# Changing the order of ranking, routing and row scoring in a product-key expert kernel, and where two normalisations end

## The reference, cut to what matters

```python
q = (xt @ w_query).reshape(t, PEER_HEADS, 2, PEER_KEY_DIM // 2)
s = jnp.einsum('thpd,hpkd->thpk', q, sub_keys)
s_half, i_half = lax.top_k(s, PEER_TOPK)                       # 16 of 128 keys, twice
cand = s_half[:, :, 0, :, None] + s_half[:, :, 1, None, :]
top_s, top_pos = lax.top_k(cand.reshape(t, PEER_HEADS, 256), PEER_TOPK)
experts = take_along_axis(cand_idx, top_pos)                   # 8 heads x 16 = 128 per token
gates = softmax(top_s)
a = gelu(einsum('tkd,td->tk', expert_u[experts], x), approximate=False)
y = einsum('tk,tkd->td', gates * a, expert_v[experts])
x = layer_norm(ALPHA * x + ga2 * y, ln2_g, ln2_b)
```

## Time and profile before

| | us |
|---|---|
| median of 3 runs | 1932.91 |
| lowest, highest | 1929.52, 1939.39 |
| the profiled execution, its own time | 1945.27 |
| its span, first to last instruction | 1943.5 |
| PE busy | 1795.4 (92%) |
| DVE busy | 1292.2 (66%) |
| POOL busy | 896.7 (46%) |
| DMA share, mean rate | 345 GB/s over the span |

### The profile page before, as it was taken

One profiled execution on the slowest core, in us unless ns is written; L12 is line 12 of the kernel. 1 busy time (PEld: TensorE's weight loads), 2 busy tenths in 40 slices (PEclk: granted clock), 3 DMA queues, 4 the chain that ended last, 5 costly groups with the idle time before them and its releaser, 6 DMA issues.

```text
span 1943.5 us, 21544 instructions
## 1 busy us (share of the span) xinstructions
PE 1795.4 (92%) x8020; PEld 1152.3 (59%) x8020; DVE 1292.2 (66%) x2593; ACT 293.5 (15%) x661; POOL 896.7 (46%) x837
## 2 busy tenths in 40 slices
PE   4988898998999999998999999996889999999994
PEld 1666743554444359987888888884554444444441
DVE  2110476989579699998998975568875623336767
ACT  0120010555100001111111100005550000000000
POOL 1010225665456324334455555668865665435540
PEclk9999999999999999998999999998999999999998
DMA  8895859888999977559999999999989999999995
GB/s 360 338 370 214 344 160 394 291 286 324 392 324 363 390 272 298 187 192 362 366 361 375 386 387 409 405 394 329 327 308 409 409 409 409 409 409 409 409 410 203
DMA packets 168441, 670.21 MB, mean 345 GB/s; under 512 B 19563, under 2 KB 19691, under 8 KB 163085
## 3 DMA queue, kind: packets, MB, share of 16 engines
q0 software_dynamic: 112512, 410.79, 56.2%
q1 hardware_dynamic: 51072, 242.25, 31.8%
q10 hardware_dynamic: 4752, 15.81, 2.1%
HBM read 659.27 MB, written 7.39 MB: 343 GB/s over the span
## 4 chain that ended last, share of the span: by engine, by line
PE 46%; DMA 18%; DVE 18%; POOL 11%; issue 6%; ACT 1%; ACTq 0%; DVEq 0%; another core or an unknown queue 0%; POOLq 0%
PE psum L966 19%; POOL arena L566 11%; DMA arena<-in_expert_u_dram,arena 9%; DMA arena<-in_expert_v_dram,arena 4%; DVE arena L1511 4%; PE psum L751 4%; PE psum L992 3%; PE psum L995 3%; DVE psum L1784 3%; PE psum L740 2%; PE psum L1029 2%; DVE arena L1707 2%; DMA arena<-in_w_ada_dram 2%; PE psum L1006 2%; PE psum L1004 2%
## 5 line engine op out<-in xcount | busy, mean ns | idle before, releaser
L566 POOL DMA_INDIRECT arena<-in_expert_u_dram,arena x384 | 468.5, 1220 | 386.0 <-DVE arena L1511 261.6
L1511 DVE CUSTOM_DVE_ANT_0 arena<-arena 128x1024 f32<-128x1024 f32 x384 | 461.0, 1222 | 182.1 <-DMA arena<-in_expert_u_dram,arena 153.0
L566 POOL DMA_INDIRECT arena<-in_expert_v_dram,arena x384 | 390.7, 1018 | 357.9 <-DVE psum L1784 175.9
L1784 DVE SCALAR_TENSOR_TENSOR psum<-arena,psum 128x1024 f32<-128x1024 f32 x254 | 327.0, 1287 | 193.2 <-DMA arena<-in_expert_v_dram,arena 165.0
L893 PE MATMUL psum<-arena 128*128 128x256 f32 x2048 | 446.0, 381 | 7.3 <-DMA arena<-in_expert_uT_dram 7.3
L966 PE MATMUL psum<-arena 128*128 128x512 f32 x1024 | 443.7, 594 | 1.6 <-DMA arena<-in_expert_v_dram 1.6
L893 PEld LDWEIGHTS psum<-arena 128*128 128x128 f32 x2048 | 390.8, 191 | 61.3 <-issue 7.6
L966 PEld LDWEIGHTS psum<-arena 128*128 128x128 f32 x1024 | 193.3, 190 | 253.0 <-issue 249.0
L1064 PE MATMUL psum<-arena 128*128 128x128 f32 x1280 | 148.9, 278 | 2.1 <-DVE arena L1668 1.4
L1064 PEld LDWEIGHTS psum<-arena 128*128 128x128 f32 x1280 | 147.1, 194 | 3.6 <-issue 1.9
L1324 ACT ACTIVATE arena<-psum 128x512 f32<-128x512 f32 x64 | 38.2, 597 | 379.7 <-PE psum L893 292.6
(11 more groups left out here) (188 smaller groups left out, 1410.1 us busy)
## 6 DMA issues: line engine op xcount, KB each, us to landing
arena<-in_expert_uT_dram SPq DMA_DIRECT2D x128, 512.0 KB
arena<-in_expert_v_dram SPq DMA_DIRECT2D x128, 512.0 KB
arena<-in_w_ada_dram SPq DMA_DIRECT2D x12, 2048.0 KB
arena<-in_w_in_dram SPq DMA_DIRECT2D x11, 2048.0 KB
arena<-in_w_query_dram SPq DMA_DIRECT2D x8, 2048.0 KB, 22.7
arena<-in_w_in_dram SPq DMA_DIRECT2D x30, 512.0 KB, 7.9
arena<-in_w_o_dram SPq DMA_DIRECT2D x4, 2048.0 KB
arena<-in_expert_u_dram,arena POOLq DMA_INDIRECT x384
```

What stands on the lines that cost most here:

```text
L566: pool.indirect_dma_start(slot, None, table[0], bass.IndirectOffsetOnAxis(ap=number, axis=0)).then_inc(land, 16)
L1511: dve.tensor_tensor_reduce(UR[b], UR[b], U2B[e], 1.0, 0.0, ALU.mult, ALU.add, DOTS[e % 2][:, k:k + 1]).then_inc(u_free, 1)
L1784: dve.scalar_tensor_tensor(ys, row, weight, ys, ALU.mult, ALU.add).then_inc(v_free, 1)
```

## The change: what it does

Tile 4 is queried, ranked and routed after tile 2. Groups of rows are dealt between 25 of the 30 steps, tile 2's own rows among them; one group is left for after the steps. The dot products of tile 2 use the buffer that held tile 1's input, so POOL loads it once tile 1 is scored. Tile 4's scores, numbers and gates lie in other buffers, so `spread(4)` comes after the whole scoring stream, the first one-hot matrix waits for it, and the last 24 blocks are scored in another order. For tiles 2 and 3 ACT scales and centres the row, and POOL multiplies and adds gain and shift.

```diff
-ORDER = (0, 1, 3, 4, 2)
+ORDER = (0, 1, 3, 2, 4)
...
-        U2B = [at(47104, D), at(44032, D), at(47104, D)]
+        U2B = [at(47104, D), at(44032, D), at(44032, D)]
...
-        HOT_J = [at(44032, BATCH, NKEYS), UT[:, :, 3 * P:4 * P]]
+        HOT_J = [at(47104, BATCH, NKEYS), UT[:, :, 3 * P:4 * P]]
...
+        DIGITS = {3: (at(0, HK), at(P, HK)), 4: (AF, BF)}
+        DGATE = {3: at(4 * P, HK), 4: GATE[1]}
...
+        def late_scores(e, qg):
+
+            if e == ORDER[-1]:
+                return UT[:, 2 * qg:2 * qg + 2, 0:2 * P]
+            return LATE[e][:, qg, :].rearrange("p (a b) -> p a b", a=2)
+
+        def scored_block(n):
+
+            i = n - KEYHALF - UPPER_PARTS
+            return n if i < 0 else KEYHALF + UPPER_PARTS + (i + 16) % 24
...
             def store_y(e):
-                sp.wait_ge(fin_step, FIN * (e + 1))
+                if e in SHARED:
+                    sp.wait_ge(tail_shifted, SHARED.index(e) + 1)
+                else:
+                    sp.wait_ge(fin_step, FIN_AT[e + 1])
...
+            def tail_gain_shift():
+
+                for i, e in enumerate(SHARED):
+                    pool.wait_ge(tail_normed, i + 1)
+                    pool.tensor_tensor(X1B[e], X1B[e], PRM2[1][1], ALU.mult).then_inc(tail_gained, 1)
+                    pool.wait_ge(tail_gained, i + 1)
+                    pool.tensor_tensor(X1B[e], X1B[e], PRM2[1][2], ALU.add).then_inc(tail_shifted, 1)
...
             routed(2)
+            score_rows(2, 0, GROUP)
+            pool.wait_ge(u_free, GROUP + 2 * HK)
             pool.dma_start(U2B[2], u2_d[2 * P:3 * P, :]).then_inc(late_u2_in, 16)
-            score_rows(2, 0, GROUP * SCORED_GROUPS)
+            score_rows(2, GROUP, GROUP * SCORED_GROUPS)
...
             last_values()
+            tail_gain_shift()
...
                 pe.wait_ge(pick_step, PICKED[e])
+                if e == ORDER[-1]:
+                    pe.wait_ge(rank_out, 2)
...
                 expert_scores(m)
+            spread(ORDER[-1])
...
             def deviation(e):
-                act.wait_ge(fin_step, FIN * e + (8 if e == ENDING[-1] else 6))
+                act.wait_ge(fin_step, FIN_AT[e] + (8 if e == ENDING[-1] else 6))
                 act.activation(RSTD[:, 0:1], MV[:, 1:2], ACT.Sqrt).then_inc(fsqrt_done, 1)
+                if e in SHARED:
+                    act.wait_ge(fin_step, FIN_AT[e] + 8)
+                    act.activation(X1B[e], X1B[e], ACT.Identity, scale=RSTD[:, 1:2], bias=MV[:, 0:1]
+                                   ).then_inc(tail_normed, 1)
...
-                if m == (KEYHALF + UPPER_PARTS) // 2:
-                    act.wait_ge(pick_step, PICKED[2])
+                if m == (KEYHALF + UPPER_PARTS) // 2 + 4:
+                    act.wait_ge(pick_step, PICKED[4] - PICKS_OF[4] + ROUTE_AT[3])
+                if m == (KEYHALF + UPPER_PARTS) // 2 + 8:
+                    act.wait_ge(pick_step, PICKED[4] - PICKS_OF[4] + ROUTE_AT[5])
...
                 expert_gelu(m)
+            take_spread(ORDER[-1])
...
                 dve.wait_ge(fin_step, base + 2)
+                if e - 1 in SHARED:
+                    dve.wait_ge(tail_normed, SHARED.index(e - 1) + 1)
                 statistics(fin_step, base + 2, x1)
...
-                normed(fin_step, FIN * e + 2, X1B[e], prm[1], prm[2], fsqrt_done, e + 1)
+                if e in SHARED:
+                    dve.wait_ge(fsqrt_done, e + 1)
+                    dve.reciprocal(RSTD[:, 1:2], RSTD[:, 0:1]).then_inc(fin_step, 1)
+                    dve.wait_ge(fin_step, FIN_AT[e] + 7)
+                    dve.scalar_tensor_tensor(MV[:, 0:1], MV[:, 0:1], -1.0, RSTD[:, 1:2], ALU.mult, ALU.mult
+                                             ).then_inc(fin_step, 1)
+                else:
+                    normed(fin_step, FIN_AT[e] + 2, X1B[e], prm[1], prm[2], fsqrt_done, e + 1)
...
                 dve.wait_ge(fin_step, base + 6)
+                dve.wait_ge(tail_normed, len(SHARED))
                 dve.bn_aggr(MV, STAT).then_inc(fin_step, 1)
...
+                if i == 0:
+                    dve.wait_ge(spread_done, len(DENSE))
                 dve.wait_ge(spread_out, d + 1)
...
+            def score_next(count):
+
+                for r in range(scored_rows[0], scored_rows[0] + count):
+                    if r == HK:
+                        dve.wait_ge(q_done, 4 * TILES)
+                        dve.memset(COLUMNS, 0.0).then_inc(zero_set, 1)
+                        dve.wait_ge(late_u2_in, 16)
+                    if r == HK + GROUP * WEIGH_AFTER:
+                        weigh(1)
+                    score(1 + r // HK, r % HK, r % HK + 1)
+                scored_rows[0] += count
+
+            steps = []
+            for e in ORDER[2:]:
+                steps += [(rank_keys, e, qg) for qg in range(4)] + [(route, e, part) for part in range(PARTS)]
+            for n, (do, e, part) in enumerate(steps):
                 do(e, part)
                 if n == FINISH_AT:
                     begin_finish(0)
                 if n == FINISH_AT + 2:
                     end_finish(0)
                 if n in DOTS_AFTER:
-                    score(1, k, k + GROUP * DOTS_AFTER[n])
...
+                    score_next(GROUP)
+            score_next(HK + GROUP * SCORED_GROUPS - scored_rows[0])
             gates()
...
+SHARED = (2, 3)
...
-SPREAD_AT = {8: 3, 24: 4}
-EXPONENTS_AT = {3: 3, 18: 4, 35: 2}
-FREED_BY_RANK = {2: 1, 20: 3, 24: 4, 28: 2}
+SPREAD_AT = {15: 3}
+EXPONENTS_AT = {11: 3, 32: 2, 55: 4}
+FREED_BY_RANK = {2: 1, 24: 3, 28: 2, 48: 4}
...
+DOTS_AFTER = (0, 1, 2, 3, 5, 7, 9, 10, 11, 12, 13, 15, 16, 17, 18, 19, 20, 21, 22, 23, 24, 25, 26, 27, 28)
+FINISH_AT, DEVIATION_AT, STORE_AT = 3, 6, 32
+NUMBERS_AT, WEIGH_AT, WEIGH_AFTER, WEIGHTS_AT = 26, 42, 3, 54
```

More of the change, by code:

```diff
@@ L1693, in rank_keys, with scored @@
                     dve.wait_ge(topk_step, 20 * si)
-                sc = LATE[e][:, qg, :] if e else bank(2 + si % 2)
+                def scored(c):
+                    if e:
+                        return late_scores(e, qg)[:, c // 2, c % 2 * P:(c % 2 + 1) * P]
+                    return bank(2 + si % 2)[:, c * P:(c + 1) * P]
                 def best(c, lo):
@@ L1701, in rank_keys @@
                     for c in range(4):
-                        src = sc[:, c * P:(c + 1) * P] if lo == 0 else SW[:, c, :]
+                        src = scored(c) if lo == 0 else SW[:, c, :]
                         dve.max(VAL[:, best(c, lo)], src).then_inc(topk_step, 1)
@@ L1873, in _ @@
             dve.wait_ge(u2_in, 16)
-            k = 0
-            for n, (do, e, part) in enumerate(
-                    [(rank_keys, 3, qg) for qg in range(4)] + [(route, 3, part) for part in range(PARTS)]
-                    + [(rank_keys, 4, qg) for qg in range(4)] + [(route, 4, part) for part in range(PARTS)]
-                    + [(rank_keys, 2, qg) for qg in range(4)] + [(route, 2, part) for part in range(PARTS)]):
+            scored_rows = [0]
+            def score_next(count):
[12 more added lines that the diff above has]
+            for n, (do, e, part) in enumerate(steps):
                 do(e, part)
@@ L1906 @@
 FIN = 9
+SHARED = (2, 3)
+FIN_AT = [FIN * e - sum(a < e for a in SHARED) for e in range(TILES + 1)]
 SUB_AT = 3 + 5 * PEER_HEADS + 1
```

34 lines of the change are left out of this document (11 added, 23 removed).

## The result

| | before | after |
|---|---|---|
| median of 6 runs, us | 1929.86 | 1918.07 |
| lowest, highest | 1928.66, 1939.39 | 1912.43, 1923.42 |
| the profiled execution, its own time | 1945.27 | 1915.63 |
| its span | 1943.5 | 1913.8 |

The ratio of the times is 0.9938, with a 95% interval of 0.9917 to 0.9958: the change makes the kernel faster by 0.62%, 11.8 us at the medians. The two profiled executions lie 29.7 us apart in their spans, and about half of that belongs to the two executions and not to the change, as will be seen.

A forecast was written before the change was run, and what follows sets the result against it. The prediction took DVE's late row queue to hold up the gates stage. An earlier one-hot matrix (9.4 us) plus the tail (3.7) gave 13.1 us, 1932.2 for the profiled execution, scaled to a 1920 us median; range 1911 to 1937.

The forecast's parts named there:

- rivals A: Row cycles of 18.6 us end DVE's rows at 1326, so no change; times near 1923 to 1933, chance about 0.3.
- D: DVE's order is not the limit on the gates stage, so only the tail gains: 1929 us, chance about 0.05.
- The sum of cycles: Steps and row groups on DVE, added cycle by cycle, put DVE's last row at 1309.3 us.
- group 3: Early row group on DVE, behind step 3 and begin_finish(0); its end was put at about 908 us.
- the group of the wait: Group 16, tile 2's first: 17.7 us plus 8.4 for DVE's wait on the input load.
- the 18 single-step cycles: Row groups on DVE with one step between them, taken at 17.7 us each.
- Rival B: Dealt groups each pay a whole fetch; slower, 1972 us if all cycles cost 20.7, mostly 1938 to 1945, chance about 0.1.
- Where DVE waits next: Before the first one-hot matrix, DVE waits 5 us for spread(4) on PE, starting at 1314.3.
- the 9.4 us of the forecast: Gain from the first one-hot matrix starting at 1314.3 instead of 1323.74, carried through the value stream.
- The waits of ACT and PE: Stream waits on DVE's steps were costed at nothing, with cover of 35 us at step 26 and 21 at step 9.
- The tail: Last normalisations: tiles 2 and 3 take 4.9 us each instead of 6.74, saving 3.7 us in all.
- Rival C: POOL's products slow beside DVE, or denser gathers starve the stream; 5 to 9 us remain, 1924 to 1928, chance about 0.15.

The follow-up runs named there:

- e2: Kernel before with only the new tail of tiles 2 and 3, order and dealing as before: 1930.27 us, ratio 1.0004 to the kernel before.
- e4: Changed kernel with tile 2's last ten row groups scored after the steps, tile 4's exponents at m = 46: 1945.78 us, ratio 1.0087 to the kernel before.
- e7: Changed kernel with the tail's 128x1 product written as tensor_scalar, one tensor and a per-partition scalar: 1914.62 us, ratio 0.9919 to the kernel before.
- e10: As e7, with tile 4's residual also kept in PSUM until the last operation: 1914.77 us, ratio 0.9914 to the kernel before.
- e1: Changed kernel with the old tail, DVE alone normalising tiles 2 and 3: 1916.55 us, ratio 0.9928 to the kernel before.
- e3: Changed kernel without the row groups after steps 0 to 2, scored at the end instead: 1937.41 us, ratio 1.0042 to the kernel before.
- e8: As e3, with the first normalisation after step 5 instead of step 3: 1945.78 us, ratio 1.0081 to the kernel before.
- e9: As e3, with the first normalisation after steps 7 and 9: 1944.56 us, ratio 1.0065 to the kernel before.
- e11: As e9, with tile 3's exponents at block m = 8 instead of 11: 1932.30 us, ratio 0.9991 to the kernel before.
- e6: Changed kernel with SP's loads for the first normalisation spread between stream blocks instead of sent together: 1918.27 us, ratio 0.9923 to the kernel before.
- e12: Changed kernel with e10's tail, e6's loads, and tile 2's input loaded behind four gathers instead of eight: 1911.26 us, ratio 0.989 to the kernel before.

## Why the prediction was right, and where its terms were off

**The cause held.** DVE's queue of rows held up the gates stage; with the rows dealt between the steps it starts right behind the stream. e2 and, less the 12.2 us of its own wait, e4 show it from both sides, and rivals A and D fall: the last row ends 468.5 us after the first ranking step, and the tail alone gives nothing that can be measured.

**The sum of cycles** was 473.6 us from the first ranking step to the last row (1309.3 - 835.74), against 468.5 measured and 488.1 before. Its terms: group 3 ended 74.3 us after the first ranking step (72.3 forecast); groups 4, 5 and 11 took 19.9, 19.6 and 17.0 (19.8, 19.6, 17.2); the group of the wait took 26.3 (26.1), the wait itself 10.9 (11.8); the 18 single-step cycles averaged 17.3 (17.7), twelve of them between 16.1 and 18.0, five from 18.5 to 21.0, and 12.6 for the last. The first of these 18, the 21.0, has two steps (8 and 9, 5.4 us together) and was counted as single. Rival B needed 19.2 and falls too. The size that was a little off is the 17.7: 18 x 0.4 = 7.2 us, less the 2.0 by which group 3 was later.

**Where DVE waits next** was a miss. The forecast let DVE wait 5 us for `spread(4)`, since it left the stream's end at 1312.8, 477.1 us after the first ranking step. It came at 467.7 after, and at 468.9 in e2, with the order of before. The forecast took the stream's end from one profile, and in that one the stream started 23.4 us behind the first ranking step, where every other profile of this case has 15.5 to 17.1. So rows and stream ended together, and the order gave more than the 9.4 us of the forecast: 14.1 us by the traces of e2 and the changed kernel (482.5 to 468.4), 12.7 by their ratios (1.0004 - 0.9938 of 1930).

**The waits of ACT and PE** on DVE's steps cost nothing, as said; PE waited 6.5 us for a block, once (7.3 before).

**The tail** is the term that failed: 3.7 us forecast, 1.1 in the trace and nothing in the times. The step "a reciprocal and one 128x1 product, 0.2 us each" took 1.48 us for the second product, and L1762's like took 2.88 us for 1.40. The rule had been named in the prediction for L1762 and L1768 and set aside, as no row bore on it; e7 and e10 show that it decides, for the small product as well, which had not been counted at all. ACT's pass was 1.24 us (bound 1.4), POOL's products 2.34 and 2.35 (2.37), and no table was loaded between root and scaling. By the rule the forecast had some 2 us for the tail; it came lower because the small product was stalled as well. Rival C's first half, POOL's products slowed beside DVE, did not happen: it was DVE that waited. Nor did its second: the stream took 451.3 us, not more than the 453.6 of before.

**The total** of 13.1 us came out as 11.8, because the order gave some 3 to 5 us more and the tail some 3 less. Two errors of opposite sign stand behind it, not one sum that held: that the total came so close is in part luck. e1, which has the order without the tail, measured 0.9928, 13.9 us.

## What to carry to other kernels

Where long work and fetches share an engine's queue, deal the fetches evenly over all of it; a stretch without them isn't made up later once the DMA engines are full (e4: the last row 27.7 us later, of which at most 12.2 in a wait of its own). When an order is changed, list the waits at fixed places of the other queues again: e3, e4, e8, e9 and e11 each priced such a wait together with what they were meant to price. Before one of two chains that meet is shortened, see how much the other is behind: e6 shortened the stream alone and won nothing, e12 shortened stream and rows and won. When products are moved to GpSimd beside DVE, let DVE's instructions there read one tensor from SBUF at most, with the other factor in PSUM or as a per-partition scalar, the small ones too.

## What the runs showed of the hardware that was not expected

A DVE product of 128 x 1 with both tensors in SBUF took 1.48 us instead of 0.16 because GpSimd's 128x1024 sum was running; it ended with it. The same product with the second factor as a per-partition scalar took 0.21 us beside the same GpSimd instruction (e7), and a pair of 128x512 with one tensor in PSUM took 1.41 us (e10), as with no GpSimd at work. So for the 128 x 1 and the 128x512 alike it was the number of tensors read from SBUF that decided. GpSimd's products and sums kept their 2.34 to 2.35 us throughout.

With the gathers it is the other way round. In the changed kernel the 199 gathers issued beside `late_values` alone (L1834, one tensor in SBUF and one in PSUM) took POOL 0.93 to 0.97 us each, and the 102 issued while DVE did nothing 0.93 to 1.02. Of the 224 issued beside the dot product alone (L1547, two tensors in SBUF) 101 took longer than 1.1 us, up to 1.99, while the dot products kept their 1.2 to 1.3 us. What the longer gathers cost the kernel was not tested.
